# Two transformer blocks on one core: projection steps spread evenly over sixteen units of dilated attention, first transfers in order of use

## The reference, cut to what matters

```python
n = rms_norm(h, ln_mix_g[l])
proj = n @ w_in[l]
qa, ka, va, qb, kb, vb, ga, gb = jnp.split(proj, splits, axis=-1)
qa = rope(qa.reshape(b, s, A_HEADS, HEAD_DIM), pos)
ka = rope(ka.reshape(b, s, A_HEADS, HEAD_DIM), pos)
ya = dilated_mixture(qa, ka, va).astype(h.dtype) @ w_branch_a[l]
yb = stick_breaking(qb, kb, vb).astype(h.dtype) @ w_branch_b[l]
...
def dilated_mixture(q, k, v):
    for g, (window, dilation) in enumerate(((128, 1), (512, 4), (2048, 16))):
        sl = slice(g * A_HEADS_PER_GROUP, (g + 1) * A_HEADS_PER_GROUP)
        o, l = dilated_group(q[:, :, sl], k[:, :, sl], v[:, :, sl], dilation, window // dilation)
    o = jnp.stack(outs, axis=0)
    wts = jax.nn.softmax(jnp.stack(lses, axis=0), axis=0)
    y = jnp.sum(wts[..., None] * o, axis=0)
```

## Time and profile before

| | |
|---|---|
| median of three runs | 3851.94 us |
| the profiled execution | 3852.3 us |
| its span | 3850.1 us |
| TensorE matmuls busy | 3466.1 us, 90% |
| VectorE busy | 1959.9 us, 51% |
| ScalarE busy | 1188.5 us, 31% |
| mean granted TensorE clock over the span | 0.934 |
| HBM read | 279.07 MB |

### The profile page before, as it was taken

The page is one execution under the profiler, slowest core; times in us unless marked ns, Lnnn a source line. Parts: engine busy times, 40 slices in busy tenths (PEclk is TensorE's granted clock), DMA queues, the critical chain, the costliest instruction groups (busy, mean ns, idle before and its releaser), DMA issues.

```text
span 3850.1 us, 49948 instructions
## 1 busy us (share of the span) xinstructions
PE 3466.1 (90%) x22042; PEld 2819.0 (73%) x22042; DVE 1959.9 (51%) x2380; ACT 1188.5 (31%) x1455; POOL 76.7 (2%) x52
## 2 busy tenths in 40 slices
PE   7999998999999999698999989996977777789996
PEld 6767777787878879587888768884756665478885
DVE  5333565776354434545443554436447774754435
ACT  2224544322232223233222332223233331232223
POOL 0000000000000001001000110000000000010001
PEclk9888999999999999899999989997978898799998
DMA  3101122222322232122222222221220000022231
GB/s 147 55 29 37 44 99 88 77 99 82 105 88 92 92 105 105 44 99 82 99 92 91 81 77 99 91 88 43 77 72 3 3 3 13 33 88 94 91 105 44
DMA packets 43416, 284.38 MB, mean 74 GB/s; under 512 B 4800, under 2 KB 4928, under 8 KB 16832
## 3 DMA queue, kind: packets, MB, share of 16 engines
q1 hardware_dynamic: 43200, 281.19, 21.1%
HBM read 279.07 MB, written 2.10 MB: 73 GB/s over the span
## 4 chain that ended last, share of the span: by engine, by line
PE 71%; DVE 8%; ACT 3%; POOL 2%; issue 2%; DMA 0%; DVEq 0%; ACTq 0%
PE ps L431 62%; PE ps L2413 5%; POOL h L713 2%; DVE wl L302 1%; ACT wh L297 1%; PE ps L643 1%; PE ps L625 1%; DVE x_area L2254 1%; DVE spare_h L2226 1%; PE ps L2625 0%; DVE tmp L2070 0%; PE ps L1952 0%; PE ps L2405 0%; DVE xl L2064 0%; DVE x_area L2226 0%
## 5 line engine op out<-in xcount | busy, mean ns | idle before, releaser
L431 PE MATMUL ps<-xh,wh 128*128 128x512 f32 x2464 | 983.8, 399 | 91.9 <-DVE xl L838 41.2
L431 PE MATMUL ps<-xl,wh 128*128 128x512 f32 x2464 | 974.2, 395 | 0.0
L431 PE MATMUL ps<-xh,wl 128*128 128x512 f32 x2464 | 973.1, 395 | 0.0
L302 DVE TENSOR_TENSOR wl<-raw,wh 128x2048 fp32r<-128x2048 f32 (+3 forms) x284 | 591.4, 2083 | 440.5 <-ACT wh L297 440.2
L431 PEld LDWEIGHTS ps<-xh,wh 128*128 128x128 f32 x2464 | 469.8, 191 | 219.2 <-issue 108.9
L297 ACT CAST wh<-raw 128x2048 fp32r<-128x2048 f32 (+3 forms) x284 | 492.3, 1734 | 305.9 <-PE ps L431 300.9
L431 PEld LDWEIGHTS ps<-xh,wl 128*128 128x128 f32 x2464 | 469.6, 191 | 102.4 <-issue 2.1
L431 PEld LDWEIGHTS ps<-xl,wh 128*128 128x128 f32 x2464 | 470.6, 191 | 99.9 <-issue 2.7
L431 PE MATMUL ps<-hid_h,wh 128*128 128x512 f32 x880 | 346.4, 394 | 2.7 <-DVE wl L302 2.7
L431 PE MATMUL ps<-hid_l,wh 128*128 128x512 f32 x880 | 345.0, 392 | 0.0
L431 PE MATMUL ps<-hid_h,wl 128*128 128x512 f32 x880 | 344.9, 392 | 0.0
(11 more groups left out here) (344 smaller groups left out, 4470.7 us busy)
## 6 DMA issues: line engine op xcount, KB each, us to landing
raw<-in_up SPq DMA_DIRECT2D x88, 1024.0 KB, 4.8
raw<-in_down SPq DMA_DIRECT2D x64, 704.0 KB, 4.0
raw<-in_up_c SPq DMA_DIRECT2D x22, 1024.0 KB, 4.8
raw<-in_down_c SPq DMA_DIRECT2D x16, 704.0 KB, 4.1
raw<-in_gates SPq DMA_DIRECT2D x8, 1024.0 KB, 4.7
raw<-in_gv SPq DMA_DIRECT2D x8, 1024.0 KB, 5.0
raw<-in_gu SPq DMA_DIRECT2D x8, 1024.0 KB, 4.7
raw<-in_gout SPq DMA_DIRECT2D x8, 1024.0 KB, 4.7
```

Source lines behind the costliest of these rows:

```text
L302: nc.vector.tensor_tensor(wl[:, slot, 0:w], raw[:, slot, 0:w], wh[:, slot, 0:w].bitcast(F32), ALU.subtract).then_inc(lo_ready, 1)
L431: last = nc.tensor.matmul(out, stationary, moving, start=(fresh and q == 0), stop=(t == kt - 1 and half == per - 1 and q == 2), skip_group ...
```

## The change

It has two parts.

At the start SyncE issues chunk 0, `vec`, x in four pieces of two tiles (512 KB) each with a semaphore of its own, then chunk 1 and `const`, each of which is waited for alone: ScalarE waits before each xh for its piece (`arrived`), VectorE and ScalarE wait for `vec`, and the sums on TensorE and the scale on VectorE for `const`. TensorE waits for none of them at its start. VectorE splits chunk 0 first. The multiplication of gains by 0.5 stands behind qa on VectorE, and ScalarE doesn't wait for it.

In the dilated stage the 96 steps are numbered through; unit u takes steps 6u to 6u + 5, two in each of the three gaps, whatever lot they belong to. A lot is evicted in the unit in which it ends, and a chunk split in the unit in which the even lot before it begins.

```diff
--- before.py
+++ after.py
@@ -766,7 +766,8 @@
 
 
         def __init__(self, gain, post=None, source=None, split=x_split, tokens=EVERY, keep=None, summed_before=False,
-                     total=None, here=None, stat=0):
+                     total=None, here=None, stat=0, arrived=None):
+            self.arrived = arrived
             self.here = here
             self.gain, self.source, self.split, self.tokens = gain, h if source is None else source, split, tokens
             self.keep = rs if keep is None else keep
@@ -795,6 +796,8 @@
             for t in range(KD):
                 if self.post:
                     self.post.wait_result(act, t)
+                if self.arrived:
+                    self.arrived(act, t)
                 nc.scalar.activation(self.split(t)[0], self.source[:, t, self.tokens], ACT.Copy,
                                      scale=vec[:, self.gain + t:self.gain + t + 1]).then_inc(n_high.sem, 1)
 
@@ -847,9 +850,13 @@
                     self.two.sum_squares(dve, t)
 
         def scale_dve(self, dve):
+            if self.arrived:
+                dve.wait_ge(const_here, 16)
             self.two.invert(dve)
 
         def sum_pe(self, pe):
+            if self.arrived:
+                pe.wait_ge(const_here, 16)
             self.two.sum_up(pe)
 
         def spread_pe(self, pe):
@@ -1057,18 +1064,25 @@
         return part
 
 
+    pair_here = [sem(f"x{n}_here") for n in range(KD // 2)]
+
+    const_here = sem("const_here")
+
+    def x_here(engine, t):
+        engine.wait_ge(pair_here[t // 2], 16)
+
     @block.sync
     def _(sp):
         load(sp, 0)
+        sp.dma_start(vec[:, :], io["vec"]).then_inc(loaded, 16)
+        for n in range(KD // 2):
+            sp.dma_start(h[:, 2 * n:2 * n + 2, :], io["x"][:, 2 * n:2 * n + 2, :]).then_inc(pair_here[n], 16)
         load(sp, 1)
-        sp.dma_start(h[:, :, :], io["x"]).then_inc(loaded, 16)
-        sp.dma_start(vec[:, :], io["vec"]).then_inc(loaded, 16)
-        sp.dma_start(const[:, :], io["const"]).then_inc(loaded, 16)
+        sp.dma_start(const[:, :], io["const"]).then_inc(const_here, 16)
 
     @block.tensor
     def _(pe):
         pe.sem_inc(chunks_used, 2)
-        pe.wait_ge(loaded, 48)
 
     @block.vector
     def _(dve):
@@ -1076,18 +1090,14 @@
         dve.sem_inc(psum_read.sem, 2)
         dve.sem_inc(dve_steps.sem, 8)
 
-        dve.wait_ge(loaded, 48)
-        halves = vec[:, VEC["norm"]:VEC["norm"] + 16 * KD].rearrange("p (a n) -> p a n", n=4 * KD)[:, :, KD:2 * KD]
-        nc.vector.tensor_scalar(halves, halves, 0.5, None, ALU.mult).then_inc(halved, 1)
-        dve.wait_ge(halved, 2)
         split_lo(dve, 0, 0, SLOT)
+        dve.wait_ge(loaded, 16)
 
     @block.scalar
     def _(act):
         act.sem_inc(act_steps.sem, 8)
         split_hi(act, 0, 16, 0, SLOT)
-        act.wait_ge(loaded, 48)
-        act.wait_ge(halved, 2)
+        act.wait_ge(loaded, 16)
 
     qk = area("qk", [P, 4 * GROUPS, T], 0)
     va = area("va", [P, TB, GROUPS * GH * HD], 24 * KB)
@@ -1097,7 +1107,7 @@
     tables_here = fetch([(rope[:, :, :], io["rope"]), (dil[:, :, :], io["dil"])], "attention_tables")
 
     rope_scaled = sem("rope_scaled")
-    first_norm = Deferred(VEC["ln_mix"])
+    first_norm = Deferred(VEC["ln_mix"], arrived=x_here)
 
     def rotate(first_tile):
         def part(dve, k, products, u):
@@ -1121,6 +1131,12 @@
         return part
 
     linear("qa", KD, 256, x_split, dve_part=rotate(0), steps=(0, 6), norms=first_norm)
+    @block.vector
+    def _(dve):
+        halves = vec[:, VEC["norm"]:VEC["norm"] + 16 * KD].rearrange("p (a n) -> p a n", n=4 * KD)[:, :, KD:2 * KD]
+        nc.vector.tensor_scalar(halves, halves, 0.5, None, ALU.mult).then_inc(halved, 1)
+        dve.wait_ge(halved, 2)
+
     linear("ka", KD, 256, x_split, dve_part=rotate(2 * GROUPS), steps=(0, 6))
     linear("va", KD, 256, x_split, act_part=to_tokens(va, first_norm, TB), token_blocks=range(TB))
 
@@ -1184,11 +1200,14 @@
 
 
 
-    beside = {}
-    for u in range(len(units)):
-        if units[u][1]:
-            n = len(beside)
-            beside[u] = ((qb_rows, kb_rows, vb_tokens)[n // 4], n % 4)
+    LOTS = [(rows_of, unit) for rows_of in (qb_rows, kb_rows, vb_tokens) for unit in range(4)]
+    PER = len(LOTS) * KD // len(units)
+
+    def ended(u):
+        return LOTS[u * PER // KD:(u + 1) * PER // KD]
+
+    def begun(u):
+        return LOTS[(u * PER + KD - 1) // KD:((u + 1) * PER + KD - 1) // KD]
 
     @block.tensor
     def _(pe):
@@ -1230,21 +1249,21 @@
             last.then_inc(da_out.sem, 1)
 
         def fill(u, t0, t1):
-            if u in beside:
-                rows_of, unit = beside[u]
-                rows_of.products(pe, unit, t0, t1)
+            for n in range(u * PER + t0, u * PER + t1):
+                rows_of, unit = LOTS[n // KD]
+                rows_of.products(pe, unit, n % KD, n % KD + 1)
 
         scores(0)
         for u in range(len(units)):
             if u + 1 < len(units):
                 scores(u + 1)
-            fill(u, 0, 3)
+            fill(u, 0, 2)
             pe.wait_ge(da_norm.sem, da_norm.after(u, 1))
             turn(u, 0)
             turn(u, 1)
-            fill(u, 3, 6)
+            fill(u, 2, 4)
             turn(u, 2)
-            fill(u, 6, 8)
+            fill(u, 4, 6)
             weigh(u)
 
     @block.vector
@@ -1289,13 +1308,13 @@
             normalise(u)
             if u + 1 < len(units):
                 mask(u + 1)
-            if u in beside:
-                rows_of, unit = beside[u]
+            for rows_of, unit in ended(u):
                 if rows_of is not vb_tokens:
                     rows_of.evict(dve, unit)
             low(u)
-            if u in beside and unit % 2 == 0:
-                rows_of.low(dve, unit // 2)
+            for rows_of, unit in begun(u):
+                if unit % 2 == 0:
+                    rows_of.low(dve, unit // 2)
 
     @block.scalar
     def _(act):
@@ -1318,15 +1337,15 @@
                 c0 += n
             if u + 1 < len(units):
                 exps(u + 1)
-            if u in beside:
-                rows_of, unit = beside[u]
+            for rows_of, unit in ended(u):
                 if rows_of is vb_tokens:
                     rows_of.evict(act, unit)
             rows, cols = slice(HD * (j % 2), HD * (j % 2) + HD), slice(b * P, (b + 1) * P)
             act.wait_ge(da_out.sem, da_out.after(u, 1))
             nc.scalar.copy(ya_h[rows, j // 2, cols], ps[rows, 7, 0:P]).then_inc(da_high.sem, 1)
-            if u in beside and unit % 2 == 0:
-                rows_of.high(act, unit // 2)
+            for rows_of, unit in begun(u):
+                if unit % 2 == 0:
+                    rows_of.high(act, unit // 2)
```

## The result

The changed kernel takes 3823.73 us (median of four runs, 3818.34 to 3827.86) against 3851.02 us for the kernel before in the same comparison: 27.3 us less, a ratio of 0.9927 with a 95% interval of 0.991 to 0.9944. A second, longer comparison gave 3820.01 against 3849.79 us, 0.9924 (0.9909 to 0.994). The profiled execution was the fastest of the four, 3818.34 us with a span of 3816.2: 34.0 us under the profiled one of before. By the spans, 10.1 us of it lie ahead of the dilated stage, 20.0 in it and 3.8 behind it. Behind it the instructions are the same; over all traces of this document, that part takes between 3509.8 and 3521.2 us, so the 3.8 say nothing of the change.

The account below looks back on a forecast made before the run. TensorE bounds the kernel, losing time by starting late, standing idle and running at its low clock. From 3852.3 us, 7.2 less at the start and 18.8 less in the dilated stage give 3826 us; 8 in 10 within 3813 to 3838.

Parts of the forecast that it names:

- The start: Kernel start: VectorE splits the first chunk at 7.6 us, TensorE starts at 10.7; 7.2 us less, bounds 0 and 8.9.
- Idle: Dilated stage: TensorE idle 5.8 us against 12.6, with two new 2.5 us waits for probs behind units 2 and 10.
- The low clock: Dilated stage: 51.2 us at the low clock instead of 75.1, costing 24.3 us.
- (a): Dilated stage's beginning: the first low-clock stretch shortens from 23.9 to about 13.7 us, as steps follow the second scores.
- (b): Dilated stage, units with b = 0: the three low-clock stretches of about 13.7 us go, with steps on both sides.
- (c): Dilated stage, four long scores (b = 3): each may drop the clock for one to two times 3.4 us; 20.5 us.
- (d): Dilated stage, two new waits for probs behind short scores: low clock of 6.8 us each, 13.6 us together.
- (e): Dilated stage: one more low-clock stretch of 3.4 us, since no more than two steps stand together.
- rival 1: Dilated stage: clock stays full once up, no fall without a long wait; stage 170.0 us, time 3809; chance 0.10.
- 3: Dilated stage: clock stays low between thin steps, 130 us of it; stage 228.1 us, time 3867, slower; chance 0.03.
- Rival 2: Dilated stage: clock falls as much as before, for 75 us; stage 199.4 us, time 3838; chance 0.16.
- Rival 4: Kernel start: a late piece or second chunk leaves 3 us gain, time 3830, or nothing, 3833.5; chance 0.06.

Follow-up runs that it names:

- e6: Changed kernel, but x loaded in one transfer in the same place; first matmul at 13.11 us, single execution 3821.34 us.
- e9: Changed kernel run again without any edit; its six runs go from 3813.04 to 3829.83 us.
- e3: Changed kernel with VectorE's split of a weight chunk one unit later, behind that unit's masks, first comparison; 3807.15 us, ratio 0.99.
- e10: Changed kernel with the weight chunk split one unit later, behind the masks, second comparison; 3809.36 us, ratio 0.9889.
- e2: Kernel before with only the even spread of steps in the dilated stage, start as before; 3830.84 us, ratio 0.9942.
- e8: Changed kernel with all six steps of a unit together behind the scores, none between the lots of transposes; 3831.96 us, ratio 0.9954.
- e7: Changed kernel, but the second weight chunk ahead of vec and x as before; first matmul at 11.92 us, single execution 3834.55 us.
- e11: Changed kernel with the late split and four of the first unit's steps ahead of the first and second scores, first comparison; 3804.78 us, ratio 0.9886.
- e12: Same kernel as e11 (late split, early steps against the changed kernel), run once more; 3797.95 us, ratio 0.9861.
- e4: Changed kernel with the two steps behind a unit's scores moved between its three groups of scores; 3840.3 us, ratio 0.9981.
- e5: Changed kernel with steps between the groups of scores and the weight chunk split one unit later; 3826.26 us, ratio 0.9947.

## Why the prediction was right

**The start** was right by each step: pieces of x land while VectorE splits the chunk (split at 7.59, I had 7.6), first matmul at 10.69 (10.7), second chunk cast behind xh, third chunk in time. The DMA term by the rate of 420 KB per us holds nearly: `vec` needs 5.1 us and lands at 6.2 (6.3 as worked out), x's pieces need 5.9 to 8.0 us, and the last lands at 11.4 (11.1 as worked out), the second chunk at 13.9 (13.5). From the landing of `vec` on, the four pieces take 5.1 us, and the same x in one transfer, in e6, 5.0. The Trainium skill ("DMA: Bandwidth & Descriptors", section Bandwidth) asks for 1 MiB or more per DMA; of queued transfers of 512 KB that isn't borne out here. A fixed cost of 2 us for each piece in turn, by which the prediction had the second chunk some 8 us later, isn't to be seen. What I left out of the sum is the clock at the start: 3 us more in this trace, of which my bound (8.9) held 1.7, and less in most others (e9's stage begins 8.1 us earlier than before's, this one's 10.1).

**Idle** was right: 5.7 us, I had 5.8, with both new waits at their places and 2.4 and 2.3 us long for 2.5. The price read from the split before a unit with b = 0 carried over. e3 and e10 show that the waits come from the split.

**The work at the full clock** stayed: 157.3 us before, 157.0 and 156.5 after.

**The low clock** was right in sum (51.2 forecast, 47.8 in the trace; 64.9 in another) and wrong in its parts. By the windows above: (a) the first stretch, 13.7 forecast, 10.2; (b) the three long ones are gone, as forecast; (c) in scores for b = 3, 20.5 forecast, 13.7, again in two of four (27.3 in e9, in all four); (d) behind the new waits, 13.6 forecast, 3.4: one fall at 167.6, none at unit 11 (two of 3.4 us in e9, none in e2); (e) 3.4 forecast for all else, 20.5 measured, of which 17.1 in the scores for the four units with b = 2 or right behind them (20.5 in e9). That last is the step that failed, and (d) was twice too large at the least. I took the fall for a matter of the longest scores and didn't look at what stands ahead of them. Scores for b = 2 come right behind a unit with b = 0, which has 2.85 us of scores and the shortest weighing (0.8 us); in seven of the eight traces of the new order with steps behind the scores (after, e9, e3, e10, e2, e8, e7) a fall comes in or right behind the scores for each of units 6, 10 and 14 (counted from 0), in the eighth, e6, for 6 and 14 but not for 10, and in e11 and e12 these three are nearly all that is left. Before the change these scores stood in the long stretches that had begun at b = 0 (187.80:201.30 in the earlier trace rows), so the trace couldn't show what they do by themselves.

So the forecast of 3826 was near the measured 3823.7 by errors that cancelled, and that is luck: the clock's share was spread over the wrong causes, and its sum was met in an execution that was the fastest of its four. The two theories I then made of it both fell (e4, e5). What fits all runs is that idle time and matmuls over 32 rows both thin out the dense ones over 128 rows, and that neither alone decides; that is a reading, and no run here measures it by itself. No run takes the scores out of the stage either, so a share of the small matmuls of the transposes and the weighing in it is not excluded. The clock page of the Trainium skill ("TensorE: Matmul & The Clock Gate", section Why this matters for your kernels) names gaps without work. The trace agrees at b = 0 of the old order, where two of the three long stretches begin within a us of a wait of 2.2 us; but in e3 nine stretches begin in 175 us without any gap, so for this stage the rule is too narrow; rival 1, which it stood for, did not come. Why the same order has 44.4 us in one execution and 64.9 in another stays open; I didn't try to steer it.

**The rivals.** 1 and 3 didn't come: 47.8 us is neither 13.7 nor 116. Rival 2 (75 us, 3838) is what the unluckier executions move towards: 64.9 us, 3829.83. Rival 4 is excluded by the start's rows.

## What to carry to other kernels

Independent products belong first where TensorE waits for other engines; here a little of them everywhere was worth 19 us more than much of them in most places (e2). Then look at what else stands on the queue of the engine that is waited for (here a 2.3 us split ahead of the probabilities), which gave another 11 us when moved behind what TensorE needs next. Give each consumer a wait for what it alone reads, in the order in which it reads. And split a stage's time into work at the full clock, idle and low clock before judging one trace: over the five traces of the changed order the idle time repeats to 0.1 us and the work to a us, and the low clock moves by 20 us. And look at where among its kernel's runs a profiled execution lies: e10 and e11 are 15.2 us apart by their profiled executions and 4.6 by their medians.

## What the runs showed of the hardware that I had not expected

The clock falls in a stage in which TensorE is busy without a gap and some of its matmuls use 32 rows: in e3 175 us without idle time had a granted clock of 0.84. The order in which the work starts has a long reach: with two steps ahead of the first scores and two behind them, not one but all three stretches at the stage's beginning stayed away, in both traces (10.2 and 13.7 us of low clock in the stage, against 41.0 and 58.0 in e10 and e3); the median moved by less, 4.6 us in the same comparison. Changing between matmuls over 32 and over 128 rows costs about 0.17 us each time, an estimate from 10 us in e4's stage. And two executions of one kernel differ by 8 us in a stage of 190 with every wait the same.
